# Value pages one place further forward in the page-load list of a decoder-step kernel

## The reference

```
z = x @ w_in                                  # queries, keys, values, scan input u, gates
s = einsum(q, k) * HEAD_DIM ** -0.5 + bias    # per head two maps
p = softmax(s);  p_diff = p[map 0] - lam * p[map 1]
attn = rms_norm(p_diff @ v) * (1 - lam_init)
ssm = s5_branch(u)                            # complex diagonal scan, GELU, GLU
h = layer_norm(alpha * x + (gate_a * (attn @ w_proj_attn) + gate_s * (ssm @ w_proj_ssm)) @ w_out)
y = layer_norm(alpha * h + conv_ffn(h))
```

## Time and profile before

| | |
|---|---|
| median of three runs | 1620.43 us (1620.25 to 1622.11) |
| the profiled execution, its own time | 1621.65 us |
| its span | 1619.6 us |
| PE busy | 1607.0 us, 99% |
| DVE, ACT, POOL busy | 1162.3, 697.6 and 442.1 us |
| bytes moved by DMA | 391.89 MB |
| mean DMA rate | 242 GB/s over the span, 376 to 401 GB/s in the slices of rounds 1 to 6 |

### The profile page before, as it was taken

One profiled execution on the slowest core, in us unless ns is written; L12 is line 12 of the kernel. 1 busy time (PEld: TensorE's weight loads), 2 busy tenths in 40 slices (PEclk: granted clock), 3 DMA queues, 4 the chain that ended last, 5 costly groups with the idle time before them and its releaser, 6 DMA issues.

```text
span 1619.6 us, 31766 instructions
## 1 busy us (share of the span) xinstructions
PE 1607.0 (99%) x11896; PEld 1452.1 (90%) x11896; DVE 1162.3 (72%) x1802; ACT 697.6 (43%) x1063; POOL 442.1 (27%) x387
## 2 busy tenths in 40 slices
PE   9999999999999999999999999999999999999998
PEld 8988777776777776999999999999999999999998
DVE  5797888887887944867778977676777776555463
ACT  4423344343443323333446844444444444334353
POOL 1187778777787710000008400000000000000000
PEclk9999999999999999999999999999999999999999
DMA  9879999999999978766665675766666675766662
GB/s 256 262 265 309 356 384 401 386 391 391 376 387 395 375 269 268 190 177 188 176 184 137 182 205 155 208 165 192 172 181 183 171 193 150 202 184 182 183 181 71
DMA packets 472393, 391.89 MB, mean 242 GB/s; under 512 B 23655, under 2 KB 436356, under 8 KB 472277
## 3 DMA queue, kind: packets, MB, share of 16 engines
q1 hardware_dynamic: 401628, 323.33, 65.0%
q10 hardware_dynamic: 70656, 67.11, 12.7%
HBM read 385.30 MB, written 5.46 MB: 241 GB/s over the span
## 4 chain that ended last, share of the span: by engine, by line
PE 94%; DMA 2%; DVE 1%; SPq 1%; POOL 1%; issue 0%; ACT 0%; ACTq 0%; DVEq 0%
PE bank L863 22%; PE bank L1304 19%; PE bank L1303 19%; PE bank L1311 19%; PE bank L843 3%; DMA work<-in_cache_v 1%; PE bank L1050 1%; PE bank L810 1%; PE bank L1076 1%; PE bank L1061 1%; PE bank L892 1%; PE bank L902 1%; PE bank L893 1%; PE bank L927 1%; PE bank L939 1%; PE bank L928 1%
## 5 line engine op out<-in xcount | busy, mean ns | idle before, releaser
L1762 ACT ACTIVATE weights_hi<-weight_ring 128x2048 fp32r<-128x2048 f32 (+1 forms) x166 | 309.7, 1866 | 457.4 <-PE bank L1304 322.2
L2323 DVE TENSOR_TENSOR weights_lo<-weight_ring,weights_hi 128x2048 fp32r<-128x2048 f32 (+1 forms) x166 | 371.0, 2235 | 104.4 <-ACT weights_hi L1762 68.7
L863 PE MATMUL bank<-work,weight_ring 128*128 128x264 f32 x1760 | 418.2, 391 | 0.3 <-ACT work L1445 0.3
L863 PEld LDWEIGHTS bank<-work,weight_ring 128*128 128x128 f32 x1760 | 325.4, 190 | 73.3 <-issue 20.9
L729 POOL TENSOR_TENSOR work<-work 128x512 f32<-128x512 f32 x256 | 324.0, 1295 | 79.4 <-DMA work<-in_cache_k 71.6
L1303 PE MATMUL bank<-h_hi,weights_hi 128*128 128x264 f32 x1184 | 291.6, 284 | 0.0
L1304 PE MATMUL bank<-h_lo,weights_hi 128*128 128x264 f32 x1184 | 290.9, 284 | 0.0
L1303 PEld LDWEIGHTS bank<-h_hi,weights_hi 128*128 128x128 f32 x1184 | 223.1, 188 | 0.0
L1304 PEld LDWEIGHTS bank<-h_lo,weights_hi 128*128 128x128 f32 x1184 | 222.7, 188 | 0.0
L2150 DVE TENSOR_REDUCE work<-work 128x8 f32<-128x512 f32 x256 | 162.6, 675 | 26.5 <-POOL work L729 26.5
L1303 PE MATMUL bank<-hidden_hi,weights_hi 128*128 128x264 f32 x688 | 169.6, 284 | 0.0
(11 more groups left out here) (340 smaller groups left out, 2497.3 us busy)
## 6 DMA issues: line engine op xcount, KB each, us to landing
weight_ring<-in_w_up SPq DMA_DIRECT2D x86, 1024.0 KB, 5.6
work<-in_cache_k SPq DMA_DIRECT2D x128, 512.0 KB, 7.7
work<-in_cache_v SPq DMA_DIRECT2D x128, 512.0 KB, 7.6
weight_ring<-in_w_in ACTq DMA_DIRECT2D x60, 1024.0 KB, 14.0
weight_ring<-in_w_down SPq DMA_DIRECT2D x32, 1024.0 KB, 6.1
weight_ring<-in_w_out SPq DMA_DIRECT2D x16, 1024.0 KB, 6.0
weight_ring<-in_w_down SPq DMA_DIRECT2D x16, 704.0 KB, 4.8
weight_ring<-in_w_proj_attn SPq DMA_DIRECT2D x16, 512.0 KB, 4.1
```

Of the source, the lines that this page charges most:

```text
L863: last = pe.matmul(bank[(n + m) % 2][:, 0:N], chunk_weight(g, k - c * per, m), tiles[k], start=(k == 0), stop=(k == len(tiles) - 1))
L1762: act.activation(w_hi[:, (j % 2) * KT * P:(j % 2) * KT * P + k_tiles * P].bitcast(F32R), slot3(j, 0, k_tiles).rearrange("p k m -> p (k m)" ...
L2323: dve.tensor_tensor(w_lo[:, cols].bitcast(F32R), slot3(off % SLOTS, 0, k_tiles).rearrange("p k m -> p (k m)"), w_hi[:, cols], ALU.subtract ...
```

## The change

Only the list changes. V1, V2, V3, V5, V6, V7 and V9 to V12 each go ahead of the key page that stood right in front of them (K5, K6, K7, K9, K10, K11 and K12 to K15), V2 so also ahead of Sv, and V13 goes ahead of the two key pages N0 and N1. V0, V4 and V8, which had no key page right in front of them, keep their place among the key pages.

```
-                for what in ("Sk", "P14", "P15", "V0", "K5", "V1", "K6", "Sv", "V2", "K7", "V3", "Bias", "K8", "Q", "V4", "K9",
-                             "V5", "K10", "V6", "K11", "V7", "V8", "K12", "V9", "K13", "V10", "K14", "V11", "K15", "V12",
-                             "N0", "N1", "V13", "N2", "N3", "N4"):
+                for what in ("Sk", "P14", "P15", "V0", "V1", "K5", "V2", "K6", "Sv", "V3", "K7", "Bias", "K8", "Q", "V4", "V5", "K9",
+                             "V6", "K10", "V7", "K11", "V8", "V9", "K12", "V10", "K13", "V11", "K14", "V12", "K15", "V13",
+                             "N0", "N1", "N2", "N3", "N4"):
```

## The result

| | before | after |
|---|---|---|
| median, runs on the same chip | 1621.25 us (9 runs, 1618.44 to 1626.02) | 1625.64 us (9 runs, 1624.36 to 1631.26) |
| ratio of the times | | 1.0034, 95% interval 1.0025 to 1.0043 |
| the profiled execution, its own time | 1621.65 us | 1625.04 us |
| its span | 1619.6 us | 1622.9 us |

A forecast was written before the change was run, and what follows sets the result against it. PE, with 94% of the chain, was taken as the bound, DMA also full in the rounds. Round 3's 1.4 us saving is given back and key pages cost 1.7: 1620.43 + 1.7 = 1622.1 us, range 1619.0 to 1627.8.

The forecast's parts named there:

- the first rival: DVE's `all_max` reaches PE's `global_max` late in every round; a 3.0 us key-page delay costs 7.2 us, 1627.6 us; chance 0.24.
- What bounds the kernel: PE has 94% of the chain, DMA is full too; PE waits 4.7 us for value pages, POOL 71.6 for key pages.
- How a page's landing moves: In the DMA queue, swapped neighbours swap landing times: K13 and K15 land 1.65 us later; 3.0 and 4.3 at the high end.
- Part 1: PE's stalls for value pages 5 and 7 in round 3 shrink, saving 1.4 us; at most 0.2 more elsewhere.
- The third rival: Nothing moves: DMA takes loads from a deep queue and stalls differ from run to run; 1620.4 to 1621 us; chance 0.18.
- Part 2: Key pages 1.65 us late exceed the spare time at `global_max`, chiefly in round 6, where the whole delay counts: 1.7 us.
- Part 3: Round 3's 1.4 us saving is given back by round 6, as the full DMA engines don't follow PE; PE ends 1.7 us later.
- Edits at nothing: On SP's queue, K6 and Sv waiting for V2, and N0 and N1 behind V13, cost nothing; nothing else queues behind these waits.
- Rule against trace: DMA turn-taking with weight chunks could cost a moved key page two places, 3.3 us; the sum kept the traced 1.65.
- Rivals 2 and 3: Rival 2: value pages' gain stays and key delays are covered, 1.6 to 2.6 us saved, 1618.8 to 1617.8 us; chance 0.14.
- those for "right": K13 multiplied some 1.6 us later, no page-5 wait over 1 us in round 3, round 6 `global_max` gap 1 us, others near 61.37.
- those for "wrong": `global_max` waits over 1 us in rounds 1 to 5, none in round 6, or key pages' issue-to-landing times staying at 10 us.

The follow-up runs named there:

- before again: The kernel before, unchanged, profiled a second time in a single run: 1620.26 us.
- e3: Kernel before with only the middle moves, V5 ahead of K9, V6 of K10, V7 of K11: 1620.08 us, 0.9998 of the kernel before.
- e12: Kernel before with only V10 moved ahead of K13: 1624.90 us, 1.0040 of the kernel before.
- e2: Kernel before with only the early moves, V1 ahead of K5, V2 of K6 and Sv, V3 of K7: 1623.21 us, 1.0011 of the kernel before.
- e10: Whole change, with POOL's last table of a round made ahead of key page 13 instead of 14: 1623.90 us, 1.0025 of the kernel before.
- e9: Whole change, with value pages 14 and 15 loaded in their own round ahead of N3, not in the next round's list: 1624.49 us, 1.0028 of the kernel before.
- e4: Kernel before with only V12 moved ahead of K15: 1623.47 us, 1.0017 of the kernel before.
- e6: Kernel before with only the seven free moves, V1, V3, V5, V7, V9, V11 and V13: 1619.97 us, 1.0002 of the kernel before.
- e5: Kernel before with only the four waiting moves, V2 ahead of K6 and Sv, V6 of K10, V10 of K13, V12 of K15: 1629.60 us, 1.0058 of the kernel before.

## Why the range of the prediction held and its likeliest outcome did not come

The range, 1619.0 to 1627.8 us, held the time. The likeliest outcome, a change of 0.2% or less, did not come. What came is the first rival, the key chain as the bound of every round, though at a smaller price than its 7.2 us. The range held because it reached up to this rival; the forecast's own sum, +1.7 us, did not come out.

- **What bounds the kernel** stood. The asymmetry of the waits was the right thing to look at: POOL's 71.6 us became 79.5, and they reached PE.
- **How a page's landing moves, the step that failed.** The prediction took one place, 1.65 us, for K13 and K15, "since K15 would have 8.1 us from its issue to that landing". In the whole change K13 lands 3.1, 3.5, 1.3, 2.5 and 1.4 us later in rounds 1 to 5, and `page_max` starts 3.0, 2.9, 1.3, 2.5 and 1.4 us later, 2.2 on the mean. The small figures of rounds 3 and 5 come from the profile of before and not from the change: there K13 landed late by itself, 39.7 and 39.2 us into the round, where the second profile of before has 37.4 in both. Beside that second profile K13 is 3.1 us later on the mean, and its issue is 3.0 us later. From issue to landing K13 took 8.0 us on the mean with the change, 7.9 in before again and 8.1 in e3: the time did not shrink, and the later issue was passed on whole, the high end given and not the value taken. K13 did not land where V10 had (39.6 to 40.2 us into the round) but at 40.9. Nor was the queue ahead of it as deep as "some five others": when K13 of round 5 was issued, three page loads were under way. For K15 the swap of places came nearer: it lands at 47.1, V12 before at 46.4 to 46.8, and its time from issue to landing shrank from 10.9 to 7.9 us in round 5. With V10's move alone, e12, K13 lands at 40.2, 1.7 us later than in the shown profile of before and 2.5 later than in the second. What makes it 40.9 in the whole change isn't shown: neither the early nor the middle part moved `page_max` when alone. That stays open.
- **Part 1**, 1.4 us saved in round 3. The mechanism held: V7 lands 1.6 us earlier in e3, as one place of 1.65 says, and the stalls for pages 5 and 7 are gone wherever V5 and V7 are moved (but for one of 0.68 us in e10). Its size was read from one execution: in the second profile of the kernel before there are two stalls for page 7, 1.26 and 0.52 us, which made their rounds 1.2 us longer together, and e3, with these moves alone, gave no gain that can be measured, 0.9998 (0.9990 to 1.0007). The third rival was half right: not the stalls, but their size differs from run to run.
- **Part 2**, the spare time at `global_max` of 1.43 to 1.72 us in rounds 1, 2, 3 and 5 and 0.5 in round 6. It differs from execution to execution as well: 1.13, 2.12, 3.26, 1.73 and 1.12 us in the second profile. At 2.2 us on the mean, not 1.65, each of rounds 1 to 5 waits, 0.6 to 1.0 us, instead of round 6 alone. That in round 6 "the whole delay counts" failed too: `page_max` came 1.4 us later there, but `all_max` only 0.4 (61.3 us after the `global_max` before it, where it was 60.9), since `page_max`'s first instruction took 0.42 us and not 1.41 (last section). Rival 1's own sum, 5d - 6.8 + (d - 2.56) - 1.4, gives +2.4 us at d = 2.2, near the 2.2 us between the two shown profiles, but by luck. It is the price of one door, which cost 3.3 us; the waits for page 15, some 1.8 us net in the six rounds, stand behind it and are in no term; and what went away in round 3 was 2.5 us, not 1.4.
- **Part 3**, that the saving is given back and PE is where the key pages let it be. The profile agrees: from round 1 on `all_max` ends only 0.15 to 0.17 us ahead of PE's multiplication, in each round. The sign of the sum, plus, came out right, its size, 1.7 us, too small by 2.7.
- **Edits at nothing.** "K6 and Sv now wait for V2" is not quite nothing: the early part alone costs 0.11% (0.02 to 0.20), and not by the key chain. "Nothing else queues behind these waits on SP" was wrong: N3, N4 and, behind them, P14 and P15 wait for K14 and K15 to be summed, and PE then waits for page 15 in six rounds. In e9 that wait was taken away without gain, since `global_max` was late by as much; in e4, where `global_max` was in time, it and the waits for pages 5 and 7 are all the loss that the profile shows. N0 and N1 behind V13, a free move, cost nothing in e6.
- **Rule against trace.** In round 5 of the changed kernel K13 lands at 511.9 and K15 at 518.5: four places in 6.6 us, 1.65 a place as before, with the weights' loads under way on ACT's queue. The Trainium skill, DMA: Bandwidth & Descriptors, "Queues, rings and completion order", has each DMA engine take turns between the queues that have work. A loss of up to two places by that, 3.3 us, would fit K13's 3.1 us; but the issue that was 3.0 us later fits it too, and no run here tells the two apart.
- **Rivals 2 and 3.** The value pages' waits stayed at 4.7 us in the profile, page 15 taking the place of 5 and 7, and no gain could be measured in any kernel, so 2 fell. Rival 3, nothing moves, holds for the seven free moves as far as can be measured.
- **The signs.** Of those for "right" two came, no wait for page 5 and a later K13; the gap before `global_max` in round 6 was 0.34 us and no wait, and round 4 was 1.1 us over 61.37. Of those for "wrong" all three came in part: one wait at `global_max` of over 1 us (round 5), none in round 6, and K13's time from issue to landing that stayed, though at 8 and not at 10 us.

## What to carry to other kernels

In a list of loads that one engine issues in order and with waits, ask of each moved entry which wait it brings along and whose loads then stand behind it: passing an entry that is free at once cost nothing here; passing one that waits cost 0.17% for the last key page of a sample and 0.40% for K13, although three to five page loads were still under way ahead, and nothing for K10 in mid-round, whose lateness did not reach the end of the chain. Follow a late load to every consumer, the later loads that wait for its place among them: here it reached PE at `global_max`, at value page 15 and, less surely, at page 7, and closing one of these gained nothing that could be measured. So judge a cause by adding it alone to the kernel before as well as by taking it away from the changed one.

## What the runs showed of the hardware

The landings of page loads scatter: V7 lands 29.2 to 33.1 us into rounds 1 to 5 in one profile of the kernel before and 29.8 to 31.5 in the other, with issues at 21.4 to 21.8 in both. PE waited 4.7 us for value pages in the one and 1.8 in the other, and the kernel's times go from 1618.0 to 1624.3 us in 32 runs on one chip. The size of a stall read from one profile is worth a second look before it goes into a sum.

`page_max`'s first instruction, an addition on DVE (L2156), takes 0.42 us or up to 1.5, by what POOL does. In the changed kernel, rounds 4 and 5:

```profile
459.40 7.60 POOL L729 TENSOR_TENSOR work<-work 128x512 f32<-128x512 f32 x6 [0.63 <-DMA work<-in_cache_k]
459.52 1.43 DVE L2156 TENSOR_TENSOR work<-work 128x256 f32<-128x256 f32 x1
...
521.98 7.70 POOL L729 TENSOR_TENSOR work<-work 128x512 f32<-128x512 f32 x6 [0.76 <-DMA work<-in_cache_k]
```

At 459.52 one of POOL's multiplications, 1.27 us each, had begun 0.12 us before, and DVE's addition ended 0.28 us after it. At 521.97 none was under way, and the addition took 0.42. All executions of L2156 in all profiles fit this: 0.42 to 0.43 us where POOL was between multiplications, else until 0.28 us behind the end of the one under way. Where POOL went straight on from K15 to the next key page, as in rounds 1 to 6 of e4, e5 and e12, it was 0.75 us, so up to 0.7 us of the delay of `page_max` did not reach `all_max` there.

In e2, once, ACT stood 9.14 us on the issue of one load of weights, and the next such issue took 5.44 us. ACT's queue and the instruction behind it, and then PEld, where this ended:

```profile
497.33 9.48 ACTq L441 DMA_DIRECT2D weight_ring<-in_w_in  x1
506.85 0.21 ACT L1445 ACTIVATE work<-conv_and_ln_parameters 128x2 f32<-128x2 f32 x1 [9.14 <-issue]
...
511.60 5.44 ACTq L441 DMA_DIRECT2D weight_ring<-in_w_in  x1
```

```profile
520.40 0.30 PEld L1102 LDWEIGHTS bank<-work 128*128 128x128 f32 x2 [2.64 <-ACT work L1445]
```

An issue that takes so long holds all of ACT's work behind it, and PE's wait was 2.3 us longer than the usual gap of 0.33. Why this issue was slow isn't known; nothing in this kernel's list bears on ACT's queue. More was lost than the wait: after it PE went on at half the granted clock for 3.4 us, which cost another 1.7, so that this round took 65.36 us. The same happened in e5 about its wait of 2.95 us in round 4, for 6.8 us, which cost 3.4. Both in windows (PE, PEld, DVE, ACT, POOL busy, PEclk, DMA share, GB/s), e2 and e5:

```profile
521.50:525.00 3.50, 3.50 (x10) 2.68 (x9) 3.43 (x7) 0.81 (x3) 1.82 (x2) 0.51 1.07 372
```

```profile
438.00:444.50 6.50, 6.24 (x22) 4.48 (x23) 3.22 (x6) 2.78 (x8) 3.96 (x4) 0.50 1.04 396
```

A PEclk of 0.5 is the lower of the clock's two levels, 1.2 GHz of 2.4. No other profile has such a stretch between the first and the last `global_max`. The mean granted clock of whole runs points the same way: the slowest run of the change (1631.26 us), of e12 (1630.23), e9 (1636.22) and e6 (1625.01) had 0.996 to 0.998, where the other runs of these kernels had 0.999 or 1.0. So a long stall of PE can cost more than itself.
